# Twelve expert steps with paired small experts, and eight neighbouring weight rows to a partition

## The reference

```python
h = modulate(rms_norm(x, norm2_g[l]), m[3], m[4])
x = x + m[5] * moe_ffn(h, router_w, router_b, moe_w1[l], moe_w3[l], moe_w2[l])

def moe_ffn(h, router_w, router_b, w1, w3, w2):
    scores = sigmoid(t @ router_w);  biased = scores + router_b
    # the best of 4 groups of 4 experts, and in it the best 2 experts of each token
    ...
    y = gates[:, 0:1] * ((silu(t @ w1[0]) * (t @ w3[0])) @ w2[0])
    for e in range(1, 16):
        y = y + gates[:, e:e+1] * ((silu(t @ w1[e]) * (t @ w3[e])) @ w2[e])
```

## Time and profile before

| | |
|---|---|
| median of 3 runs | 928.34 us (925.67 to 930.66) |
| the profiled execution | 927.07 us, of which the span of instructions 925.2 |
| PE busy | 865.7 us (94%), 3803 matmul records |
| DVE, ACT, POOL busy | 383.7, 197.6, 122.8 us |
| granted PE clock, mean | 0.970 |
| expert weights | 32 transfers of 1024.0 KB and 32 of 512.0 KB |
| all of `q1` (issued by SP) | 122.61 MB |
| routed rows, in and out, `q0` (GpSimd) | 8.40 MB |

### The profile page before, as it was taken

One profiled execution on the slowest core, in us unless ns is written; L12 is line 12 of the kernel. 1 busy time (PEld: TensorE's weight loads), 2 busy tenths in 40 slices (PEclk: granted clock), 3 DMA queues, 4 the chain that ended last, 5 costly groups with the idle time before them and its releaser, 6 DMA issues. The chain is left out here.

```text
span 925.2 us, 9791 instructions
## 1 busy us (share of the span) xinstructions
PE 865.7 (94%) x3803; PEld 459.7 (50%) x3803; DVE 383.7 (41%) x805; ACT 197.6 (21%) x435; POOL 122.8 (13%) x109
## 2 busy tenths in 40 slices
PE   4999999999999999999999999999993899999993
PEld 3445476655844445555555554444553444444441
DVE  3239455643345426556675750102236322222221
ACT  3221266100011032322332320100120222111110
POOL 1000000000148300110111111110001022221211
PEclk9899999999999999999999999999985899999997
DMA  8952020300072134262533435205142489999952
GB/s 313 330 193 91 0 91 1 115 1 1 1 250 76 39 99 153 91 205 60 184 98 134 147 136 198 91 0 182 45 168 83 155 269 300 299 305 289 308 148 41
DMA packets 79234, 131.65 MB, mean 142 GB/s; under 512 B 7297, under 2 KB 40786, under 8 KB 79186
## 3 DMA queue, kind: packets, MB, share of 16 engines
q1 hardware_dynamic: 74578, 122.61, 38.9%
q0 software_dynamic: 4608, 8.40, 4.0%
HBM read 126.79 MB, written 12.58 MB: 151 GB/s over the span
## 5 line engine op out<-in xcount | busy, mean ns | idle before, releaser
L468 PE MATMUL ps<-arena 128*128 128x512 f32 (+9 forms) x2962 | 770.6, 451 | 15.1 <-DVE arena L1593 5.7
L468 PEld LDWEIGHTS ps<-arena 128*128 128x128 f32 (+5 forms) x2962 | 360.3, 167 | 375.9 <-issue 355.2
L1022 ACT ACTIVATE arena<-ps 128x512 f32<-128x512 f32 (+5 forms) x132 | 54.7, 439 | 180.3 <-PE ps L468 133.3
L471 PE MATMUL ps<-tab,arena 128*128 128x128 f32 x476 | 67.4, 285 | 14.5 <-DVE arena L1266 6.6
L471 PEld LDWEIGHTS ps<-tab,arena 128*128 128x128 f32 x476 | 58.0, 148 | 42.7 <-issue 34.3
L1436 DVE SCALAR_TENSOR_TENSOR arena<-arena,ps 128x512 f32<-128x512 f32 x32 | 22.0, 687 | 116.7 <-ACT arena L1111 116.5
L1761 POOL TENSOR_TENSOR arena<-arena 128x512 f32<-128x512 f32 x24 | 30.4, 1268 | 279.8 <-DVE arena L1436 279.8
L1726 POOL TENSOR_TENSOR stat<-stat,mhalf 128x1 f32<-128x1 f32 (+2 forms) x20 | 23.2, 1162 | 319.0 <-DVE stat L1241 318.9
L1111 ACT ACTIVATE arena<-ps 128x512 f32<-128x512 f32 x32 | 19.1, 597 | 198.9 <-PE ps L468 198.9
L1684 DVE TENSOR_TENSOR arena<-arena,ps 128x256 f32<-128x256 f32 x16 | 6.7, 422 | 105.5 <-ACT arena L1213 105.5
L1404 DVE SCALAR_TENSOR_TENSOR arena<-arena,cond 128x512 f32<-128x512 f32 x56 | 42.6, 761 | 2.3 <-PE ps L471 0.6
(11 more groups left out here) (149 smaller groups left out, 379.0 us busy)
## 6 DMA issues: line engine op xcount, KB each, us to landing
arena<-in_moe_w SPq DMA_DIRECT2D x32, 1024.0 KB, 10.3
arena<-in_w_in SPq DMA_DIRECT2D x12, 2048.0 KB, 8.9
arena<-in_mod_w SPq DMA_DIRECT2D x16, 1024.0 KB, 5.2
arena<-in_moe_w SPq DMA_DIRECT2D x32, 512.0 KB, 10.7
arena<-in_mod_w SPq DMA_DIRECT2D x4, 2048.0 KB, 16.8
arena<-in_w_out SPq DMA_DIRECT2D x2, 2048.0 KB, 7.9
arena<-in_x SPq DMA_DIRECT2D x4, 512.0 KB, 5.7
arena<-in_w_in SPq DMA_DIRECT2D x2, 1024.0 KB, 18.3
```

The lines of the kernel that those rows point to most:

```text
L468: return nc.tensor.matmul(o, l, r, start=start, stop=stop, skip_group_check=True)
L471: return nc.tensor.transpose(o, i, ident[0:n, 0:n])
L1022: return A_(o, i, ACT.Copy)
```

## The change

The number of steps falls from sixteen to twelve. Experts 0 and 1 keep their own steps. The other 14 are ranked by their token count on the chip: the six largest get a step each (steps 2 to 7), the eight smallest are put in pairs into steps 8 to 11, the first of a pair in places 0 to 63, the second in places 64 to 127. An expert of a pair may have 64 tokens; if more, the kernel runs a further round of sixteen steps for the rest. DVE computes the ranking (`order_by_count`, `place_columns`) and rearranges positions and gates by it (`permute`); SP reads the expert numbers from the on-chip memory (`eid`) and loads 14 experts by them. There are six places for weights instead of four, and only experts 0 and 1 are loaded before the lists exist.

In a paired step each of the 12 large matmuls is two: 64 columns of the stationary operand, to output partitions 0 to 63 and 64 to 127, each with its own expert's weights as the moving operand.

Row `8*p + k` of w1, w3 and the router's weights now goes to partition p, slot k: one piece is eight neighbouring rows, 8 KB (512 B for the router). So that features agree, `xn2` is stored in that order of columns, and the second norm's gain and the two modulation vectors it uses are brought into it (`cols2_in`, and eight matmuls instead of four in four of the eight `mod_sum`).

```diff
+HALF_CAP = P // 2
+KNOWN = 2
+SINGLE = 8
+STEPS = SINGLE + (NE - SINGLE) // 2
+FREE = NE - KNOWN
+SLOTS = 6
+TOKEN_GROUPS = [(0, 2), (2, 4), (6, 4), (10, 2)]
+def step_parts(s):
+    if s < SINGLE:
+        return [(slice(0, P), s)]
+    return [(slice(0, HALF_CAP), s), (slice(HALF_CAP, P), s + (NE - SINGLE) // 2)]
+LOAD_COLUMNS = [c for s in range(STEPS) for _, c in step_parts(s)]
...
             def load_expert(q, e):
                 e = bass.ds(e, 1)
-                sp.dma_start(w13[q][:, 0], A["moe_w1"][0, e].rearrange("e (k p) f -> p (e k) f", p=P)).then_inc(moe_in[q], 16)
+                sp.dma_start(w13[q][:, 0], A["moe_w1"][0, e].rearrange("e (p k) f -> p (e k) f", k=KD)).then_inc(moe_in[q], 16)
...
-                if t == XT - 1:
-                    for n in range(N_OUT, N_LOADS):
-                        sp.wait_ge(ring_used[n % RING], used_value(n))
-                    load_expert(2, 2)
...
-            sp.wait_ge(hg_in[1], 16)
-            load_expert(3, 3)
-            def weights(r, first=0):
-                with sp.Fori(first, NE // 4) as i:
-                    for q in range(4):
-                        sp.wait_ge(y_mm, NE * r + 4 * i + (q - 3))
-                        load_expert(q, 4 * i + q)
+            sp.wait_ge(sort_ready, 1)
+            for n in range(KNOWN, NE):
+                if n == KNOWN:
+                    for m in range(N_OUT, N_LOADS):
+                        sp.wait_ge(ring_used[m % RING], used_value(m))
+                if n == SLOTS - 1:
+                    sp.wait_ge(out_done, 16 * XT)
+                e = expert_of(LOAD_COLUMNS[n])
+                if n >= SLOTS:
+                    sp.wait_ge(y_mm, load_step(n - SLOTS) + 1)
+                load_expert(n % SLOTS, e)
...
+                if m // 2 in (1, 2):
+                    rows_of = slice(m % 2 * HD, (m % 2 + 1) * HD)
+                    for k in range(KD):
+                        col = KD * (m // 2) + k
+                        last = mm(ps[rows_of, 5, col:col + 1], mod_acc(m).rearrange("p (n k) -> p k n", k=KD)[:, k, :],
+                                  const("ones")[:, 0:1], True, True)
...
+            def hidden(parts, slots):
+                for k in range(KD):
+                    for (rows_of, c), q in zip(parts, slots):
+                        last = mm(ps[rows_of, 2, :].rearrange("p (w f) -> p w f", w=2), hgT[:, k, rows_of], w13[q][:, :, k, :],
+                                  k == 0, k == KD - 1)
+                last.then_inc(h_mm, 1)
+            def outputs(par, parts, slots):
+                for half in range(2):
+                    for f in range(2):
+                        for (rows_of, c), q in zip(parts, slots):
+                            last = mm(ps[rows_of, 4 + 2 * par + half, :], aT[:, f, rows_of], w2[q][f][:, half * 512:(half + 1) * 512],
+                                      f == 0, f == 1)
+                last.then_inc(y_mm, 1)
...
-                V.tensor_scalar(xn2[:, t], xr[:, t], stat[:, 32 + t:33 + t], None, ALU.mult).then_inc(xn2_done, 1)
+                V.tensor_scalar(xn2[:, t].rearrange("p (k n) -> p k n", k=KD), xr[:, t].rearrange("p (n k) -> p k n", k=KD),
+                                stat[:, 32 + t:33 + t], None, ALU.mult).then_inc(xn2_done, 1)
...
+            def first_experts():
+                make_first_picks(0, KNOWN)
+                order_by_count()
+                take_first_tokens(0)
+                place_columns()
+                permute(tE(posP)[:, :, KNOWN:NE], tE(posm))
+                ...
+                dve.wait_ge(hg_mm, 1)
+                modulate()
+                permute(gateP.rearrange("p (t e) -> p t e", t=XT), gate[:, :, :])
+                split_gates(gateP.rearrange("p (t e) -> p t e", t=XT), KNOWN, FREE)
+                make_first_picks(*TOKEN_GROUPS[1])
```

More of the change, by code:

```diff
@@ new lines, in experts, with pick_columns, turn_expert, outputs_expert @@
+            def experts(r):
+                whole = [(slice(0, P), None)]
+                pe.wait_ge(aT_ready, done(r))
+                def pick_columns(first, count):
+                    for c in range(first, first + count):
+                        f = c // 4
+                        if c % 4 == 0 and f >= 1:
+                            pe.wait_ge(tok_ready, 4 * r + f)
+                        pe.wait_ge(pick_ready, done(r) + c + 1)
+                        picks(f, c, [(slice(0, P), c)])
+                def turn_expert(i, o):
+                    pe.wait_ge(hg_in[o % 2], 16 * nth_of_two(r, i, o))
+                    turn_tokens(o % 2)
+                def outputs_expert(i, o):
@@ L939, in step @@
                     pe.wait_ge(hgT_act, nth(r, i, o))
                     pe.wait_ge(hgT_dve, nth(r, i, o))
-                    for k in range(KD):
-                        last = mm(ps[:, 2, :].rearrange("p (w f) -> p w f", w=2), hgT[:, k, :], w13[o % 4][:, :, k, :],
-                                  k == 0, k == KD - 1)
-                    last.then_inc(h_mm, 1)
-                    if o == 0:
-                        picks(12, 4)
+                    hidden(whole, [o % 4])
                     if not is_last(i, o):
-                        turn_tokens(i, o + 1)
+                        turn_expert(i, o + 1)
@@ new lines, in _, with take @@
+            tok_sum = rt[:, 600:604]
+            def take(f, count, got, first, ready):
+                V.tensor_reduce(tok_sum[:, 0:count], got[:, :, 0:2], AX.X, ALU.add).then_inc(tok_step, 1)
+                V.tensor_reduce(gate_of[:, first:first + count], got[:, :, 2:5], AX.X, ALU.add).then_inc(gate_take, 1)
+                dve.wait_ge(tok_step, ready)
+                V.tensor_scalar(tok_of[:, first:first + count], tok_sum[:, 0:count], float(NOBODY), None, ALU.add).then_inc(tok_ready, 1)
+                dve.wait_ge(tok_ready, ready)
@@ new lines, in take_first_tokens @@
+            def take_first_tokens(f):
+                first, count = TOKEN_GROUPS[f]
+                dve.wait_ge(pick_mm, first + count)
+                got = ps[:, (7 if f else 3), 5 * first:5 * (first + count)].rearrange("p (e c) -> p e c", c=5)
+                take(f, count, got, first, f + 1)
+            key, order_of, key2, column = (rt[:, a:a + FREE] for a in (1536, 1824, 1568, 1584))
+            wide = [P, FREE, FREE]
+            compare = rt[:, 1840:1840 + FREE * FREE].rearrange("p (e j) -> p e j", e=FREE)
@@ new lines, in experts @@
+            def experts(r):
+                for par in range(2):
+                    dve.wait_ge(hg_in[par], 16 * done_of_two(r))
+                    dve.wait_ge(ys_out[par], 16 * done_of_two(r))
+                V.tensor_scalar(posP, posP, -float(CAP), None, ALU.add).then_inc(shift_done, 1)
+                dve.wait_ge(shift_done, r)
+                def make_picks(first, count):
+                    for c in range(first, first + count):
+                        dve.wait_ge(pick_mm, done(r) + (c + 1 - PICKS))
+                        one_hot(pick[:, c % PICKS], tE(posP)[:, :, c:c + 1], P).then_inc(pick_ready, 1)
+                def take_tokens(f):
+                    dve.wait_ge(pick_mm, done(r) + 4 * (f + 1))
+                    got = ps[:, (7 if f else 3), 20 * f:20 * f + 20].rearrange("p (e c) -> p e c", c=5)
+                    take(f, 4, got, 4 * f, 4 * r + (f + 1))
```

395 lines of the change are left out of this document (257 added, 138 removed).

## The result

The changed kernel takes 904.73 us (median of 4 runs, 903.26 to 907.56) against 928.96 us (925.67 to 930.66) of the kernel before: ratio 0.9747, 95% interval 0.9711 to 0.9783. It is 24.2 us faster; the forecast was 906 us, with 888 to 923 as its range.

The account below looks back on a forecast made before the run. PE bounds the expert part's first half, with transfers almost level and taking over once PE's work falls. Expert part -26.5, pairs +0.5, clock +2.5, modulation sums +1.5, `xn2` +0.3: -21.7 us, so 906 us, range 888 to 923.

Parts of the forecast that it names:

- less than half of PE's 45.6 us comes back: Expert part: four dropped steps free 4 x 11.40 = 45.6 us of PE, but transfers limit the gain to -21.7.
- Pairs: Paired steps: two half-wide matmuls run as one, 0 to 1.7 us more per step, 0.3 taken.
- Rival (b): Paired steps: the two matmuls run one after the other, 21.7 us a step, about 925 us; chance 0.12.
- (a): Expert part: transfers are quick, PE and places decide; last weights at 855.5, 893 us; chance 0.13.
- Start of the loads: After the lists: picks from 705.39, ranking done at 710.5, first byte of expert weights at 713.5.
- The trunk: Before the experts: four of eight `mod_sum` have eight matmuls instead of four, +0 to +3.8 us, 1.5 taken.
- `xn2`: Trunk: `xn2` reads every eighth number, only the last tile counts, 0 to +0.75 us, 0.3 taken.
- The rate: Expert loads: 50.8 MB with routed rows at 330 GB/s, 154 us, last weights at 868.5.
- Rival (c): Expert loads: long pieces bring nothing, 304 GB/s, last weights at 881.6, 13.1 later, 919 us; chance 0.09.
- The tail and the clock: From hidden of the last expert: 30.2 us before, plus 0.5 for pairs and 2.5 for clock after waits of 8 to 12.

Follow-up runs that it names:

- the swap: Changed kernel, with DVE taking the next group's tokens before the modulation instead of after it: 901.25 us, ratio 0.9731.
- the spread places: On top of the swap, the places of a whole step's list spread over all 128 partitions instead of filled from the bottom: 896.11 us, ratio 0.9658.

## Why the prediction was right, point by point

**Right in kind.** It said that the forecast's mechanism would be: transfers, not PE, set the end, and less than half of PE's 45.6 us comes back. Half the bytes moved the start of step 11 by 11 to 13 us, so transfers do have a part of that size in the end. "Less than half" is met only in the profiled execution, the slowest of the four, with 19.5 of 45.6 us; by the medians 24.2 came back, a little over half.

**Pairs.** Forecast +0.3 a step, measured 11.69 - 11.40 = +0.29. Rival (b) is out. So is (a) for this kernel: it put step 11 at 855.5, 143.8 us after the forecast issue at 711.7, and 153.8 and 152.3 were measured. With the swap and the spread places 144.9 and 143.6 are reached, so (a) described a kernel that was two edits away.

**Start of the loads.** The chain was right: ranking done 5.05 us after the first pick, forecast 5.1, and the issue came 1.0 us later. Its place in time was not: the first load was issued at 720.47, where 711.7 plus the trunk's 1.8 was forecast, so it came seven us too late.

**The trunk is the step that was mis-sized.** "+0 to +3.8, I take 1.5" stood on "half as wide weight loads could halve each". The row that it rested on was contiguous. Each reordered sum costs 1.3 (2.08 against 0.95, and 0.2 in what surrounds it), 5.3 for four, outside my bound; 1.7 more went to a fall of the clock of which I had no term. `xn2` was right: 1.14 instead of 0.75, +0.39, forecast +0.3. Together 7.4 for 1.8; the other 1.7 of the shift of 9.1 us at the router's matmuls is there at 37 us already, and the very start differs by 1.5 us between the two profiles of the changed kernel.

**The rate.** Forecast 154 us plus 1 from the first byte, 156.8 from the issue; measured 153.8 and 152.3. The 50.8 MB thus moved at about 334 GB/s, forecast 330. This agreement is in part luck. The forecast took 330 for what the transfers can do beside routed rows. In fact they did 417 GB/s while loads were queued and 289 in the hollow behind the late steps 1 and 2, and in between they were asked for 338, the pace at which places came free. The spread places with the swap held 393 to 415 GB/s from 734 to 770 us, with routed rows among them, where the prediction held against (a) that no such stretch came near 386. How much of the 153 us is the transfers' own speed and how much is waiting for places is not separated. Rival (c) spoke of what long pieces bring: with 1 KB pieces it takes 158.9 us. They bring 5 to 7 us here, not 13, and not nothing. At 417 GB/s for 12 us, nothing stopped the long pieces near the rate of 1 KB pieces. This is against the rule of the Trainium skill (DMA: Bandwidth & Descriptors, Where 436 GB/s comes from) that a limit near 358 GB/s binds, at least with one core at work.

**The tail and the clock.** +3.0 forecast, +1.2 measured: 905.7 - 874.31 = 31.4 us against 30.2. The clock was lower at the start of step 11 as said (0.50 from 876 to 878 us), but the waits ahead of steps 10 and 11 are 4.1 us each and not "8 to 12". PE came late instead: step 8 began at 827.59, not at 811.3, since the trunk and steps 1 and 2 (9 us) had held it up, and so it had less left to wait.

**What was missed**: the two waits of 2 us in steps 1 and 2, with half-clock matmuls behind each, from DVE's order and the gathers. The places were missed too: they hold the issues from the fifth load on, where the forecast looked only at the last two loads and took their places to be free in time.

**The sum.** From 903.5 of span forecast to 905.7: loads start +7.0, from first issue to step 11 -3.0, tail -1.8. The forecast was near because three errors partly cancel, which is luck; by its steps it was right on the pairs and the ranking, right on the rate's number but not on what set it, and wrong on the trunk.

## What to carry to other kernels

When a change takes work from one engine in a part where another is almost level, work out how long the other needs alone, from its first byte on, and beside it when each buffer comes free for the next transfer: here neither alone gave the end (starting the loads earlier at the cost of PE's first step gained nothing). A layout that makes transfers longer must be paid for somewhere: find each operand that is then read with a stride, and give the stride to an engine that has slack. And where a gather puts short lists into the lower partitions only, try spreading them over all: here that took 5 us off the median and raised the traffic by 7 and 22% in two stretches.

## What the runs showed of the hardware

- A stationary operand read at every eighth number (32 bytes apart) costs 233 ns a record of 128 columns in matmuls with one moving column; the contiguous one 119 to 122. With 64 columns read at the same stride it is 2.08 / 16 = 130 ns.
- Behind 2 to 4 us of matmuls with one moving column and a strided operand the granted clock fell to 1.2 GHz although PE was busy throughout: behind the last of the four sums of 2.08 us in every profiled kernel with them and behind none of the first three, behind each of the two of 3.73 us, and behind none of the contiguous ones, not even those of 1.95 us (which also stand in another place). What in them matters to the clock was not separated.
- Two matmuls of 512 columns with 64 stationary columns each, to different halves of the outputs and with different moving operands, run together: 7.02 us for 16 pairs of records against 6.87 for 16 whole ones.
- With w1 and w3 in 8 KB pieces the traffic, gathers and scatters included, reached 417 GB/s over 12 us with the DMA engines fully busy; with 1 KB pieces it was 349 in the same 12 us and 367 from 736 to 748 us with the places spread.
- DVE reading at every eighth number takes 1.14 us instead of 0.75 for 1024 numbers a partition.
